# A float32 transformer kernel on one core: first layer woven with weight slabs in its attention; in the second layer weights split ahead of masks

## The chip, the cores and the metric

The kernel runs on one core of one Trainium2 chip, as a single launch. Its metric is the device time in microseconds (us) of that core. The engines are TensorE (PE in the profile; its weight loads are PEld), VectorE (DVE), ScalarE (ACT), GpSimd (POOL) and SyncE (SP), which here only issues transfers. TensorE runs at one of two clocks, 1.2 or 2.4 GHz; PEclk in the profile is the share of the upper one that was granted.

## The reference, cut to what matters

Two models follow each other on 512 tokens of width 1024, two layers each. The change is in the two layers of the first model, where every matrix is float32:

```python
for i in range(2):                       # first_block
    h = rmsnorm(x, norm_mix[i])
    ...                                  # mk, mv: keys and values of 256 memory tokens
    if i % 2 == 0:                       # first layer: 12 query heads, 4 key heads, 4 memory heads
        q, k, v, qm = jnp.split(h @ w_in_a[li], [qw, qw + kvw, qw + 2 * kvw], axis=-1)
        y_tok = windowed_gqa(...)        # 4 blocks of 128 queries, up to 384 keys, ALiBi, a sink logit
    else:                                # second layer: 12 query, 12 key heads
        q, k, v, qm = jnp.split(h @ w_in_b[li], [qw, 2 * qw, 3 * qw], axis=-1)
        y_tok = neighbourhood_attn(...)  # 256 keys, a learned bias per head (rpb), a grid mask
    y_mem = memory_attn(qm, mk, mv)
    x = x + jnp.concatenate([y_tok, y_mem], axis=-1) @ w_out[i]
    ...                                  # gated FFN
```

## The kernel before, in words

Activations lie with the model's width on the partitions, so a head pair of 64 + 64 columns is one "tile" of 128 partitions by 512 tokens. A "slab" is 128 output columns of a weight matrix, all 1024 rows: 128 x 1024 float32, 512 KB. float32 products are made from rounded parts. SP brings a slab to `raw` (a ring of two slots), ACT rounds it to `w_hi` (L987), POOL subtracts to get `w_lo` (L695), each in halves of 128x512, and PE makes three products for each of the 8 row tiles: hi by hi, lo by hi, hi by lo (L1466), 24 matmuls a slab and 12 a half slab. Each engine runs its own list in order; semaphores join them.

The first layer before: a projection of 12 slabs (queries, keys, values, memory queries), then the attention in 6 tiles of 4 query blocks, 24 "steps" (a step is one block of one tile, both heads), then 8 steps of memory attention, then the output projection of 8 slabs. Slabs and steps don't mix there.

The second layer is "woven": `woven_row` puts the 8 memory steps and the 24 neighbourhood steps in one row. In step p, PE makes the scores of p, the transposes of p-2, half a slab of the projection (`woven_part`, L1694 in `products`; a tile's query slab and key slab, 4 halves in 4 steps), and the values of p-3. After step 23 the projection is used up, and `OUT_PARTS` gives the steps 24 to 31 single row tiles of the first two output slabs. ACT in step p makes the exponentials of the first head (`probs`, L1088), copies the transposes of p-1 out of PSUM (`turned_woven`, L1195), makes those of the second head, rounds y (L1170), and rounds half a slab (`split_woven`). DVE adds the bias and takes the row maximum as it reads the scores (L2013). POOL in `attend_woven` does in each step, in this order: a chore, a half of `w_lo`, and `y_lo`. The chore stages a piece of the tile that comes four steps later: its queries (L723, L725), its keys, its values (L776), or, in every fourth step, its bias with the grid mask (`mask`, L790, three instructions), which the very next step's scores take:

```python
if p.at + 4 < len(row):
    then = row[p.at + 4]
    ...
    chores[then.st][n](then.tile)
if n < 2 and 1 <= u <= W_TILES:
    split_lo(first + u, 1, UP, (n,))
if n >= 2 and u < W_TILES:
    split_lo(first + u + 1, 0, UP, (n - 2,))
```

At the head of a woven row POOL waits until DVE has emptied both accumulators (`acc_free`) and then stages the first tile.

## Time and profile before

| | us |
|---|---|
| runs of the kernel | 2647.85, 2651.76, 2651.86 (median 2651.76) |
| the profiled execution | 2646.34 |
| its span in the trace | 2644.6 |
| first layer: projection | 52 to 121.3 |
| first layer: attention, memory attention | 121.3 to 188.0, 188.0 to 209.5 |
| first layer: output projection | 209.5 to 261.6 |
| second layer: woven row | 673 to 841 |

The times of the trace are us from the span's start. A row of a timeline gives the start, the time of the group, the engine, the line, the operation and its tiles; in brackets stands how long the engine had stood before, and whose end released it. The stretches of the table are read off PE's timeline, where its lines change.

### The profile page before, as it was taken

What the parts mean: (1) busy time and instruction counts of PE and PEld (TensorE: products, weight loads), DVE (VectorE), ACT (ScalarE), POOL (GpSimd) and SP (SyncE); (2) the same over time, 40 slices, a digit from 0 to 9 for tenths busy, and PEclk for the clock granted to TensorE, in tenths of its full rate; (3) what the DMA queues carried; (4) which work ended last, traced back from release to release, by engine and by line L of the source; (5) the groups of instructions that cost most, each with busy time, mean ns of one, the idle gap of its engine ahead of it and who ended that gap; (6) DMA issues with size and microseconds to landing.
All of it is one profiled execution on the core that took longest, in us unless ns stands there. A gap on an engine that the chain in (4) does not pass through costs nothing.

```text
span 2644.6 us, 46681 instructions
## 1 busy us (share of the span) xinstructions
PE 2541.5 (96%) x16758; PEld 2196.2 (83%) x16758; DVE 959.7 (36%) x1748; ACT 919.9 (35%) x1988; POOL 1201.3 (45%) x1039
## 2 busy tenths in 40 slices
PE   7999999999999999999998979999999888999999
PEld 7767888888776888888997869999999667998897
DVE  4263221223445221226753433422432543441341
ACT  4284322232244322234242223322233565322231
POOL 4554444444565444444442534444444443444443
PEclk9999999999999999999998989999999999999999
DMA  5211232232121222232221002232222100223222
GB/s 174 80 42 64 95 103 87 91 106 83 53 63 58 92 95 99 87 107 88 83 77 41 2 20 93 87 101 78 92 93 75 33 25 33 90 93 99 92 93 97
DMA packets 59473, 209.16 MB, mean 79 GB/s; under 512 B 8544, under 2 KB 11232, under 8 KB 59360
## 3 DMA queue, kind: packets, MB, share of 16 engines
q1 hardware_dynamic: 59360, 207.66, 24.1%
q8 instruction: 70, 1.15, 0.2%
q14 instruction: 43, 0.35, 0.0%
HBM read 205.54 MB, written 2.10 MB: 79 GB/s over the span
## 4 chain that ended last, share of the span: by engine, by line
PE 90%; DVE 4%; ACT 2%; issue 2%; POOL 1%; SPq 1%; DVEq 0%; DMA 0%; ACTq 0%; POOLq 0%
PE ps L1466 74%; PE ps L1694 3%; PE ps L1660 2%; PE ps L1642 1%; PE ps L1830 1%; PE ps L1591 1%; PE ps L1619 1%; PE ps L1819 1%; DVE s_sb L2013 1%; PE ps L1481 1%; PE ps L1669 1%; PE ps L1684 1%; DVE y_sb L1988 0%; DVE s_sb L1988 0%; PE ps L1604 0%
## 5 line engine op out<-in xcount | busy, mean ns | idle before, releaser
L695 POOL TENSOR_TENSOR w_lo<-raw,w_hi 128x512 fp32r<-128x512 f32 (+1 forms) x704 | 977.4, 1409 | 1156.1 <-ACT w_hi L987 1155.7
L987 ACT ACTIVATE w_hi<-raw 128x512 fp32r<-128x512 f32 (+1 forms) x704 | 428.2, 653 | 1276.0 <-PE ps L1466 1256.5
L1466 PE MATMUL ps<-h_hi,w_hi 128*128 128x264 f32 (+2 forms) x2832 | 791.4, 329 | 11.4 <-POOL h_lo L910 8.0
L1466 PE MATMUL ps<-h_lo,w_hi 128*128 128x264 f32 (+2 forms) x2832 | 789.5, 328 | 0.0
L1466 PE MATMUL ps<-h_hi,w_lo 128*128 128x264 f32 (+2 forms) x2832 | 786.8, 328 | 0.0
L1466 PEld LDWEIGHTS ps<-h_hi,w_hi 128*128 128x128 f32 x2832 | 479.8, 189 | 64.9 <-issue 13.8
L1466 PEld LDWEIGHTS ps<-h_lo,w_hi 128*128 128x128 f32 x2832 | 476.5, 189 | 48.1 <-issue 1.0
L1466 PEld LDWEIGHTS ps<-h_hi,w_lo 128*128 128x128 f32 x2832 | 476.7, 189 | 47.2
L1466 PE MATMUL ps<-act_lo,w_hi 128*128 128x512 f32 (+1 forms) x880 | 280.5, 351 | 0.0
L1466 PE MATMUL ps<-act_hi,w_lo 128*128 128x512 f32 (+1 forms) x880 | 279.8, 350 | 0.0
L1466 PE MATMUL ps<-act_hi,w_hi 128*128 128x512 f32 (+1 forms) x880 | 278.8, 349 | 0.0
L1988 DVE TENSOR_TENSOR x<-x,ps 128x512 f32<-128x512 f32 (+3 forms) x96 | 66.6, 693 | 432.0 <-PE ps L1466 430.5
L1466 PEld LDWEIGHTS ps<-act_hi,w_hi 128*128 128x128 f32 x880 | 153.3, 188 | 24.4
L1466 PEld LDWEIGHTS ps<-act_lo,w_hi 128*128 128x128 f32 x880 | 153.6, 188 | 24.0
L1466 PEld LDWEIGHTS ps<-act_hi,w_lo 128*128 128x128 f32 x880 | 153.9, 188 | 22.7
L1988 DVE TENSOR_TENSOR ps<-gated,ps 128x512 f32<-128x512 f32 (+1 forms) x88 | 61.6, 701 | 169.4 <-PE ps L1466 169.1
L1983 DVE SCALAR_TENSOR_TENSOR ps<-padded,vec,ps 128x528 f32<-128x528 f32 (+1 forms) x132 | 101.2, 767 | 25.9 <-issue 15.5
L1988 DVE TENSOR_TENSOR act_lo<-ps,act_hi 128x512 f32 (+1 forms) x88 | 61.2, 696 | 104.3 <-ACT act_hi L1252 104.3
L1988 DVE TENSOR_TENSOR padded<-ps,rstd 128x528 f32<-128x528 f32 (+1 forms) x56 | 39.4, 703 | 154.8 <-PE ps L1466 143.6
L1983 DVE SCALAR_TENSOR_TENSOR h_lo<-x,vec,h_hi 128x512 fp32r<-128x512 f32 (+2 forms) x64 | 59.4, 928 | 81.2 <-ACT h_hi L994 68.1
L1249 ACT ACTIVATE ps<-ps 128x512 f32<-128x512 f32 (+1 forms) x88 | 51.5, 585 | 105.8 <-DVE ps L1983 105.8
L1988 DVE TENSOR_TENSOR gated<-ps,rstd 128x512 f32<-128x512 f32 (+1 forms) x88 | 61.2, 696 | 73.2 <-ACT ps L1249 73.2
(311 smaller groups left out, 2785.0 us busy)
## 6 DMA issues: line engine op xcount, KB each, us to landing
raw<-slabs_d SPq DMA_DIRECT2D x288, 512.0 KB, 3.3
raw<-slabs_d SPq DMA_DIRECT2D x64, 704.0 KB, 4.0
bias_sb<-alibi_d SPq DMA_DIRECT2D x6, 384.0 KB, 3.7
x<-x_d SPq DMA_DIRECT2D x1, 2048.0 KB, 13.5
out_d<-x SPq DMA_DIRECT2D x8, 256.0 KB, 4.4
rpb_raw<-rpb_d SPq DMA_DIRECT2D x6, 256.0 KB, 2.7
mem_in<-mem_d SPq DMA_DIRECT2D x1, 1024.0 KB, 7.2
cst<-consts_d SPq DMA_DIRECT2D x1, 792.0 KB, 9.4
```

The costliest lines, as they stand in the source:

```text
L695: nc.gpsimd.tensor_tensor(w_lo[:, s, a * P:b * P], raw[:, s, a * P:b * P], w_hi[:, s, a * P:b * P].bitcast(f32), ALU.subtract).then_inc(lo ...
L987: nc.scalar.activation(w_hi[:, s, a * P:b * P], raw[:, s, a * P:b * P], ACT.Copy)\
L1249: nc.scalar.activation(acc(2, st.used), acc(2, st.used), ACT.Silu).then_inc(silu_ready, 1)
L1466: last = nc.tensor.matmul(ps[:, s * 2 * BANK + po:s * 2 * BANK + po + n], w[:, s, wk], columns(a, k, to, n), start=(k == 0 and w is w_hi a ...
L1481: last = nc.tensor.matmul(out, a[:, k, t0:t0 + n], w[:, s, wk], start=(k == 0 and w is w_hi and a is hi), stop=(k == DT - 1 and w is w_lo))
L1591: last = nc.tensor.matmul(p.score(h)[0:p.nq, col:col + n], a[hp, p.tile_slot, p.q], b[hp, p.tile_slot, k0:k0 + n], start=(b is k_hi and a ...
L1619: last = nc.tensor.transpose(to, s_sb[0:p.nq, p.slot, h, 1 + col:1 + col + n], ident[0:p.nq, 0:p.nq])
L1642: last = nc.tensor.matmul(split_acc[:, c, :], wt[:, w.s, k * P:(k + 1) * P], a[:, k, to:to + n], start=(k == 0 and wt is w_hi and a is hi) ...
L1660: nc.tensor.matmul(out[HD * h:HD * h + HD, 0:p.nq], v_st[0:n, p.tile_slot, vb, HD * h:HD * h + HD], p_t[0:n, p.slot, h, j, 0:p.nq], start= ...
L1694: last = nc.tensor.matmul(acc(s, 1), w[:, s, k * P:(k + 1) * P], columns(a, k, META, SEQ), start=(k == first and w is w_hi and a is hi), s ...
L1983: return nc.vector.scalar_tensor_tensor(*a, **kw)
L1988: return nc.vector.tensor_tensor(*a, **kw)
```

## The change

In the first layer the projection keeps 4 slabs (two of memory queries, two of values). The rest is woven like the second layer: memory attention comes first, in steps 0 to 7, and beside it the slabs of the first two query tiles and of the two key tiles; then come the 24 windowed steps. Three query tiles share one key tile there (`group=3`), so of a tile only one query slab is left to make, which stands as two halves in the even steps. The odd steps have no slab. Output slab parts stand in steps 24 to 28 and 31 (`OUT_FIRST`), the rest behind the last step. The transposes of the second head go to another PSUM bank. In ACT's step `spread` and `move_y`, which the windowed attention needs for its sums, stand between the second head's exponentials and y.

In both layers POOL now splits its half slab ahead of the chore, waits for only one accumulator before it stages the first tile, and `OUT_PARTS` is ordered anew.

```diff
-    proj(10, 2, 1)
-    out[-1].queries = (0, 1, 2, 4)
+    proj(2, 2, 1)
+    out[-1].queries = (0,)
+    out[-1].woven = True
+    att(nt=2, blocks=m_blocks, bias=None, sink=None, qt=0, kt=0, group=1, y=6, layer=0)
+    out[-1].woven = True
+    slabs(2 * 2, UP)
     att(nt=6, blocks=a_blocks, bias="alibi", sink=0, qt=0, kt=6, group=3, y=0, layer=0)
-    att(nt=2, blocks=m_blocks, bias=None, sink=None, qt=8, kt=0, group=1, y=6, layer=0)
-    tail(2, 1, 0, False, (3, 1))
+    out[-1].woven = True
+    slabs(4, UP)
...
-        OUT_PARTS = {24: [(0, 6), (0, 7)], 25: [(0, 0), (0, 1)], 26: [(0, 2)], 27: [(1, 6), (1, 7)], 28: [(1, 0)],
-                     29: [(1, 1)], 30: [(1, 2)], 31: [(0, 3)]}
+        OUT_FIRST = {24: [(0, 0)], 25: [(0, 1)], 26: [(0, 2)], 27: [(0, 6)], 28: [(0, 7)], 31: [(0, 3)]}
+        def woven_slab(a, p):
+            first, u, n = a.slab0 // 2, p.at // 4, p.at % 4
+            if u >= W_TILES:
+                return None
+            if u < 2 or not shares_keys(a):
+                return first + u, n // 2, range(n % 2 * DT // 2, (n % 2 + 1) * DT // 2), n // 2
+            if n % 2:
+                return None
+            return first + 2 + (u - 2) // 2, u % 2, range(n // 2 * DT // 2, (n // 2 + 1) * DT // 2), 0
+        def shares_keys(a):
+            return stages[stages.index(a) + 1].group > 1
+        def out_pair(a):
+            return a.slab0 // 2 + (4 if shares_keys(a) else W_TILES)
+        def woven_splits(a, p):
+            first, u, n = a.slab0 // 2, p.at // 4, p.at % 4
+            if n < 2:
+                if u == 1 or (u <= W_TILES and u and not shares_keys(a)):
+                    return [(first + u, 1, n)]
+                return [(out_pair(a), 1, n)] if u == W_TILES else []
+            if u >= W_TILES:
+                return []
+            if not shares_keys(a) or u == 0:
+                return [(first + u + 1, 0, n - 2)]
+            return [(first + 2 + (u - 1) // 2, 1 - u % 2, n - 2)]
+        OUT_PARTS = {24: [(0, 0), (0, 1)], 25: [(0, 2)], 26: [(0, 6), (0, 7)], 27: [(1, 0), (1, 1)], 28: [(1, 2)],
+                     29: [(1, 6)], 30: [(1, 7)], 31: [(0, 3)]}
...
-                for s in range(RING):
-                    pool.wait_ge(acc_free[s], first)
+                pool.wait_ge(acc_free[0], first)
                 for n in (0, 1, 2):
                     chores[a][n](0)
+                pool.wait_ge(acc_free[1], first)
                 stream(a.slab0 + 2)
                 pool.wait_ge(val_kept, a.val0)
                 for p in row:
                     u, n = p.at // 4, p.at % 4
+                    for q, s, part in woven_splits(a, p):
+                        split_lo(q, s, UP, (part,))
                     if p.at + 4 < len(row):
                         then = row[p.at + 4]
                         if then.st is b and n < 2:
-                            pool.wait_ge(acc_free[n], first + then.tile + 1)
+                            if then.tile < 2 or not shares_keys(a):
+                                pool.wait_ge(acc_free[n], first + then.tile + 1)
+                            elif n == 0:
+                                pool.wait_ge(acc_free[then.tile % 2], first + 2 + (then.tile - 2) // 2 + 1)
                         chores[then.st][n](then.tile)
-                    if n < 2 and 1 <= u <= W_TILES:
-                        split_lo(first + u, 1, UP, (n,))
-                    if n >= 2 and u < W_TILES:
-                        split_lo(first + u + 1, 0, UP, (n - 2,))
                     if p.back(3).exists:
                         y_lo_of(p.back(3).st, p.back(3).tile, p.back(3).b)
                 for p in row[-3:]:
                     y_lo_of(p.st, p.tile, p.b)
...
+                        act.wait_ge(pv_done, p.count - 1)
+                    if p.st.sink is not None:
+                        n = len(p.c["chunks"])
+                        for h in range(2):
+                            last = nc.scalar.activation(
+                                p_t[:, p.slot, h, 0:n, :],
+                                bank(4 - 2 * h)[:, 0:n * P].rearrange("p (c n) -> p c n", n=P), ACT.Copy)
+                        last.then_inc(pt_ready[0], 1)
+                        return
...
                         probs(p, 1)
+                        if p.back(1).exists:
+                            spread(p.back(1))
+                        if p.back(2).exists:
+                            move_y(p.back(2))
                         if p.back(3).exists:
                             y_hi(p.back(3))
                         split_woven(p)
...
+                    if p.st.sink is not None:
+                        pe.wait_ge(acc_free[1], st.slab0 // 2 + 2)
                     for j, (col, n, _) in enumerate(p.c["chunks"]):
...
                 def woven_part(p):
-                    u, n = p.at // 4, p.at % 4
-                    if u >= W_TILES:
-                        out_parts(OUT_PARTS[p.at])
+                    if woven_slab(st, p) is None:
+                        out_parts((OUT_FIRST if shares_keys(st) else OUT_PARTS).get(p.at, []))
                         return
-                    q, s, half = st.slab0 // 2 + u, n // 2, n % 2
-                    if half:
+                    q, s, tiles, at = woven_slab(st, p)
+                    if tiles[0] == 0:
+                        begin(q, s)
+                        if s != at or (shares_keys(st) and p.at >= 8):
+                            pe.wait_ge(acc_free[1 - s], q + s)
+                    if tiles[0] == DT // 2:
                         second_half(q, s)
-                    else:
-                        begin(q, s)
-                    products(q, s, range(half * DT // 2, (half + 1) * DT // 2), h_hi[st.h], h_lo[st.h], 0, DT - 1)
+                    products(s, at, tiles, h_hi[st.h], h_lo[st.h], 0, DT - 1)
```

Three places show it as the engines' lists have it. POOL, second layer, step 6 to 7 (`v_st` is the values' chore of tile 0, `bias_sb` its mask, `y_w` a y_lo). Before:

```order
L776 COPY v_st<-val_w_80 128x640
L695 TENSOR_TENSOR w_lo<-raw,w_hi 128x512
L810 TENSOR_TENSOR y_w_0_82<-y_sb_w_81,y_w_0_82 128x128
L790 TENSOR_TENSOR bias_sb<-rpb_raw,cst 128x2x256
L790 TENSOR_TENSOR bias_sb<-rpb_raw,cst 128x2x192 x2
L695 TENSOR_TENSOR w_lo<-raw,w_hi 128x512
L810 TENSOR_TENSOR y_w_1_83<-y_sb_w_81,y_w_1_83 128x128
```

After:

```order
L736 TENSOR_TENSOR w_lo<-raw,w_hi 128x512
L817 COPY v_st<-val_w_60 128x640
L851 TENSOR_TENSOR y_w_0_62<-y_sb_w_61,y_w_0_62 128x128
L736 TENSOR_TENSOR w_lo<-raw,w_hi 128x512
L831 TENSOR_TENSOR bias_sb<-rpb_raw,cst 128x2x256
L831 TENSOR_TENSOR bias_sb<-rpb_raw,cst 128x2x192 x2
L851 TENSOR_TENSOR y_w_1_63<-y_sb_w_61,y_w_1_63 128x128
```

The mask was ahead of its step's `w_lo` and is now behind it; so are the other chores.

ACT, first layer, one windowed step (`p_t` is the copy of transposes, `s_sb,p_sum` the exponentials). Before:

```order
L1103 ACTIVATE p_t<-ps 128x256
L1091 ACTIVATE s_sb,p_sum<-s_sb,n_max 128x385
L1103 ACTIVATE p_t<-ps 128x256
L1091 ACTIVATE s_sb,p_sum<-s_sb,n_max 128x385
L1147 ACTIVATE p_rec<-p_inv 128x128
L1157 ACTIVATE y_sb_55<-ps 128x128
L1170 ACTIVATE h_hi_49<-y_sb_55 128x128
```

After, in a step that has half a slab:

```order
L1131 ACTIVATE s_sb,p_sum<-s_sb,n_max 128x385
L1241 ACTIVATE p_t<-ps 128x384 x2
L1131 ACTIVATE s_sb,p_sum<-s_sb,n_max 128x385
L1189 ACTIVATE p_rec<-p_inv 128x128
L1199 ACTIVATE y_sb_w_61<-ps 128x128
L1212 ACTIVATE y_w_2_64<-y_sb_w_61 128x128
L1029 ACTIVATE w_hi<-raw 128x512
```

The copies moved from between heads to ahead of the second head's exponentials, and the rounding of half a slab stands last.

PE, first layer, a windowed step (`k_hi,q_hi` are scores, `cst,s_sb` transposes, `p_t,v_st` values). Before:

```order
L1591 MATMUL ps<-k_hi,q_hi 128x256 x2
L1591 MATMUL ps<-k_lo,q_hi 128x256 x2
L1591 MATMUL ps<-k_hi,q_lo 128x256 x2
L1604 MATMUL ps<-cst,s_sb 128x128 x6
L1660 MATMUL ps<-p_t,v_st 64x128 x6
L1675 MATMUL ps<-cst,p_rec 128x128
```

After, from the last row tile of a half slab on:

```order
L1756 MATMUL ps<-h_hi_49,w_hi 128x512
L1756 MATMUL ps<-h_lo_50,w_hi 128x512
L1756 MATMUL ps<-h_hi_49,w_lo 128x512
L1716 MATMUL ps<-p_t,v_st 64x128 x4
L1731 MATMUL ps<-cst,p_rec 128x128
L1647 MATMUL ps<-k_hi,q_hi 128x256 x2
L1647 MATMUL ps<-k_lo,q_hi 128x256 x2
L1647 MATMUL ps<-k_hi,q_lo 128x256 x2
L1747 MATMUL ps<-cst,s_sb 128x128 x6
L1716 MATMUL ps<-p_t,v_st 64x128 x4
L1731 MATMUL ps<-cst,p_rec 128x128
L1647 MATMUL ps<-k_hi,q_hi 128x256 x2
```

The transposes of a step with no slab are followed at once by the values of the step before, and then the next scores.

## Rows read from the trace of the kernel before

**Rows 1.** The page, part 1: busy time of each engine, its share of the span, instructions.

```profile
PE 2541.5 (96%) x16758; PEld 2196.2 (83%) x16758; DVE 959.7 (36%) x1748; ACT 919.9 (35%) x1988; POOL 1201.3 (45%) x1039
```

**Rows 2.** Windows of the first layer: window, length, busy time of each engine (instructions), PEclk.

```profile
121.30:188.00 66.70, 61.65 (x550) 42.64 (x550) 46.54 (x171) 58.96 (x221) 40.11 (x60) 0.95 0.14 44
188.00:209.50 21.50, 16.80 (x186) 13.05 (x186) 13.94 (x22) 11.73 (x37) 4.57 (x10) 0.92 0.01 2
209.50:262.00 52.50, 52.43 (x219) 42.13 (x219) 17.06 (x24) 18.61 (x34) 24.04 (x16) 0.97 0.24 76
```

**Rows 3.** Timeline of PE, second layer, steps 8 and 9: where their scores start.

```profile
777.16 0.36 PE L1591 MATMUL ps<-k_hi,q_hi 64*128 64x192 f32 x2
...
782.07 0.39 PE L1591 MATMUL ps<-k_hi,q_hi 64*128 64x256 f32 x2
```

**Rows 4.** Timeline of POOL, second layer: a mask and the halves of w_lo behind masks.

```profile
776.66 3.22 POOL L790 TENSOR_TENSOR bias_sb<-rpb_raw,cst 128x512 f32<-128x512 f32 x3
780.27 1.28 POOL L695 TENSOR_TENSOR w_lo<-raw,w_hi 128x512 fp32r<-128x512 f32 x1 [0.39 <-ACT w_hi L987]
...
800.84 1.26 POOL L695 TENSOR_TENSOR w_lo<-raw,w_hi 128x512 fp32r<-128x512 f32 x1 [0.37 <-ACT w_hi L987]
```

**Rows 5.** Timeline of DVE, second layer, step 8: the scores' first head.

```profile
779.92 0.36 DVE L2013 CUSTOM_DVE_ANT_0 s_sb<-ps,bias_sb 128x192 f32<-128x192 f32 x1 [1.32 <-POOL bias_sb L790]
```

**Rows 6.** Timeline of ACT, second layer, step 8.

```profile
778.36 0.60 ACT L1195 ACTIVATE p_t<-ps 128x512 f32<-128x512 f32 x1 [3.15 <-PE ps L1684]
...
779.56 0.64 ACT L987 ACTIVATE w_hi<-raw 128x512 fp32r<-128x512 f32 x1
```

**Rows 7.** Timeline of PE, second layer: the stands of the row's end, and what followed.

```profile
802.36 0.70 PE L1694 MATMUL ps<-y_w,w_hi 128*128 128x512 f32 x2 [3.41 <-POOL w_lo L695]
...
803.89 0.63 PE L1694 MATMUL ps<-y_w,w_lo 128*128 128x512 f32 x1
...
806.36 0.51 PE L1591 MATMUL ps<-k_hi,q_hi 64*128 64x256 f32 x2
...
841.50 0.73 PE L1466 MATMUL ps<-y_w,w_hi 128*128 128x512 f32 x2 [1.43 <-POOL w_lo L695]
842.07 0.40 PE L1466 MATMUL ps<-y_w,w_lo 128*128 128x512 f32 x1
```

**Rows 8.** Timeline of PE at the head of the woven row.

```profile
676.26 0.39 PE L1591 MATMUL ps<-k_hi,q_hi 64*128 64x256 f32 x2 [3.55 <-POOL k_lo L725]
...
677.74 0.80 PE L1694 MATMUL ps<-h_hi,w_hi 128*128 128x512 f32 x1 [0.86 <-POOL w_lo L695]
```

**Rows 9.** Timeline of DVE at the head of the woven row: the copy of the values.

```profile
672.99 1.27 DVE L1998 COPY val_w<-ps 128x384 f32<-128x384 f32 x3
```

**Rows 10.** Timeline of POOL at the head of the woven row.

```profile
673.02 0.61 POOL L723 CAST q_hi<-ring 128x512 fp32r<-128x512 f32 x1 [9.73 <-issue]
```

**Rows 11.** Timeline of PE, first layer: one step, its values, the next scores.

```profile
137.38 0.39 PE L1591 MATMUL ps<-k_hi,q_hi 64*128 64x256 f32 x2
...
138.80 0.66 PE L1660 MATMUL ps<-p_t,v_st 128*64 128x128 f32 x8
...
139.65 0.38 PE L1591 MATMUL ps<-k_hi,q_hi 64*128 64x256 f32 x2
```

**Rows 12.** Timeline of ACT, first layer: from one step into the next.

```profile
139.69 0.50 ACT L1103 ACTIVATE p_t<-ps 128x384 f32<-128x384 f32 x1
140.06 0.63 ACT L1091 ACTIVATE s_sb<-s_sb,n_max 128x385 f32<-128x385 f32 x1
...
141.22 0.51 ACT L1103 ACTIVATE p_t<-ps 128x384 f32<-128x384 f32 x1
```

**Rows 13.** Timeline of DVE, first layer: two copies of the sink logits.

```profile
121.38 1.29 DVE L1988 TENSOR_TENSOR s_sb<-neg_rows 128x2 f32<-128x2 f32 x1
...
149.28 0.16 DVE L1988 TENSOR_TENSOR s_sb<-neg_rows 128x2 f32<-128x2 f32 x1
```

**Rows 14.** Timeline of POOL, first layer, beside the first of these copies.

```profile
121.36 2.51 POOL L695 TENSOR_TENSOR w_lo<-raw,w_hi 128x512 fp32r<-128x512 f32 x2 [1.66 <-ACT w_hi L987]
```

More of the change, by code:

```diff
@@ L837, in attend_woven @@
                     y_lo_of(p.st, p.tile, p.b)
-                streamed(2 * (first + W_TILES) + 2)
+                streamed(2 * out_pair(a) + 2)
             def attend(st, nxt, nv):
@@ L1076, in attend @@
             def attend(st):
-                off = 1 if st.sink is None else 0
                 def probs(p, h):
@@ L1140, in spread @@
                 def spread(p):
-                    if st.summed:
+                    if p.st.summed:
                         return
+                    if p.row and p.back(2).exists and p.back(2).st.summed:
+                        act.wait_ge(y_ready, p.count - 1)
                     act.wait_ge(inv_ready, p.kept + 1)
@@ L1198, in split_woven @@
                 def split_woven(p):
-                    first, u, n = st.slab0 // 2, p.at // 4, p.at % 4
-                    if n < 2 and 1 <= u <= W_TILES:
-                        split_hi(first + u, 1, UP, (n,))
-                    if n >= 2 and u < W_TILES:
-                        split_hi(first + u + 1, 0, UP, (n - 2,))
+                    for q, s, part in woven_splits(st, p):
+                        split_hi(q, s, UP, (part,))
                 if st.woven:
@@ L1215, in attend @@
                     turned_woven(last)
-                    for k in (2, 1, 0):
-                        y_hi(last.back(k))
+                    spread(last)
+                    move_y(last.back(1))
+                    y_hi(last.back(2))
+                    move_y(last)
+                    y_hi(last.back(1))
+                    y_hi(last)
                     return
@@ L1680, in turn_woven, with products @@
                     pe.wait_ge(p_ready, 2 * p.count + 2)
-                    pe.wait_ge(pt_ready[0], p.count)
+                    if counted(p.count):
+                        pe.wait_ge(pt_ready[0], p.count)
+                    if p.st.sink is not None:
+                        pe.wait_ge(acc_free[1], st.slab0 // 2 + 2)
                     for j, (col, n, _) in enumerate(p.c["chunks"]):
                         for h in range(2):
-                            last = nc.tensor.transpose(bank(4)[0:n, (2 * h + j) * P:(2 * h + j + 1) * P],
-                                                       s_sb[0:p.nq, p.slot, h, 1 + col:1 + col + n], ident)
+                            if p.st.sink is not None:
+                                to = bank(4 - 2 * h)[0:n, j * P:(j + 1) * P]
+                            else:
+                                to = bank(4)[0:n, (2 * h + j) * P:(2 * h + j + 1) * P]
+                            last = nc.tensor.transpose(to, s_sb[0:p.nq, p.slot, h, 1 + col:1 + col + n], ident)
                     last.then_inc(pt_done, 2)
                 transpose = turn_woven if st.woven else turn_both if st.mixed else turn
-                def products(q, s, tiles, hi, lo, first, end):
+                def products(s, at, tiles, hi, lo, first, end):
                     for k in tiles:
                         for w, a in ((w_hi, hi), (w_hi, lo), (w_lo, hi)):
-                            last = nc.tensor.matmul(acc(s, 1), w[:, s, k * P:(k + 1) * P], columns(a, k, META, SEQ),
+                            last = nc.tensor.matmul(acc(at, 1), w[:, s, k * P:(k + 1) * P], columns(a, k, META, SEQ),
                                                     start=(k == first and w is w_hi and a is hi),
@@ L2249, in attend @@
                         scores(p)
+                        if p.back(1).exists:
+                            invert(p.back(1))
                         evict_woven(p)
```

59 lines of the change are left out of this document (37 added, 22 removed).

## The prediction

> **What bounds the kernel now.** Read the page's first part first: PE is busy for 96% of the span [rows 1], so an edit counts only where PE stands, or where it runs at the lower clock. The windows of the first layer show where that is. In the attention PE has 61.65 of 66.70 us and ACT 58.96, so ACT nearly fills that stretch; in the memory attention PE has 16.80 of 21.50; in the output projection 52.43 of 52.50 [rows 2]. PE thus stands 5.05 + 4.70 + 0.07 = 9.8 us. The granted clocks 0.95, 0.92 and 0.97 on these lengths are (0.05 x 66.7) + (0.08 x 21.5) + (0.03 x 52.5) = 3.3 + 1.7 + 1.6 = 6.6 us more, if all of it is time. So 16.4 us is all that weaving can give back. In the second layer PE's timeline has stands only at the head of the woven row (3.55 and 0.86 us) [rows 8], once where its steps lose their half slab (3.41, released by `w_lo`) and at its end (1.43) [rows 7]. The masks cost nothing there yet: at step 8 the scores start on PE at 777.16 and those of step 9 at 782.07 [rows 3], while DVE reads the first head of step 8 at 779.92, released by the mask [rows 5]. The mask is late for DVE by 1.32, and DVE still frees the PSUM bank (779.92 + 0.36 = 780.28) 1.8 us before PE asks for it again.
>
> **Second layer: the mask behind `w_lo`.** POOL did the mask at 776.66, for 3.22 us, then waited 0.39 for ACT and made `w_lo` from 780.27, 1.28 long [rows 4]. That half cannot start sooner when it stands first: its `w_hi` starts on ACT at 779.56 and takes 0.64, and it comes behind a copy of transposes which PE makes only after the scores of the next step (ACT stood 3.15 for them, until 778.36) [rows 6]. So `w_hi` of a step ends 779.56 + 0.64 - 777.16 = 3.04 us into PE's next step, and everything behind it on POOL is later than that. The new order gives `w_lo` 780.27 to 781.55, the mask 781.55 to 784.77, DVE's first head to 784.77 + 0.40 = 785.17. PE's scores of step 9 want to start at 782.07 and use that bank: a stand of 785.17 - 782.07 = 3.1 us. What waits behind the mask on POOL is a `y_lo`, which the output needs much later; what waits behind DVE is ACT's exponentials, and by them the transposes two steps on, which have slack of a step. The stand comes for every mask made while PE still has half slabs beside it: tiles 0 to 3, so 4 x 3.1 = 12.4.
>
> Tile 4 is where the half slabs end. There the old order made PE stand 3.41 for the `w_lo` behind the mask (at 800.84) [rows 4, 7]. The new `OUT_PARTS` takes row tiles of the first half there, which is ready, so this stand goes, and the mask is late instead: with a shorter step beside it by an estimated 3.9. I take 0 for the two together. Tile 5 has no half slab behind which to stand, but its step is short; I take +1.3, from the same order of slack (1.32) [rows 5].
>
> A stand also cost clock. Behind the one of 3.41 a matmul of 128x512 took 0.63 at 803.89, behind the one of 1.43 it took 0.40 at 842.07 [rows 7]: half clock after the long one, none after the short one. From 803.89 to the scores at 806.36, which took 0.51 where 0.39 is usual [rows 3, 7], 2.47 us passed at roughly 0.40/0.63 of the speed, or half, which is 0.9 to 1.3 lost; I take 1.3. Four new stands of 3.1 are nearer to 3.41 than to 1.43: 4 x 1.3 = 5.2, with bounds 0 and, if the low clock lasts twice as long, 10.4.
>
> The head of the row gains. POOL's staging started at 673.02, after the copy of the values on DVE began (672.99, three pieces in 1.27) and nine microseconds idle [rows 9, 10]. It waited for both accumulators, and needs only the first now, which DVE empties while PE still makes the last slab. PE itself waits for the values' copy, so its scores can start about when that ends, 672.99 + 1.27 = 674.26, and after scores that take 0.7 the first product, at 677.74 before [rows 8], stands near 675.0: -2.7, and about -1 for a shorter stretch at half clock, so -3.7. It can't be sooner than the values' copy; the other bound is 0, if POOL's `w_lo` of the last slab takes the place of the wait.
>
> Sum for the second layer: 12.4 + 0 + 1.3 + 5.2 - 3.7 = +15. With the clock's bounds and the head's it is +7.5 to +20.
>
> **First layer.** The same number of slabs and steps is made, so only what PE stood counts. ACT's work per windowed step is, from two copies of transposes at 0.37 each (139.69 to 140.06), two heads of exponentials, 0.63 each, of which the second with three small ones behind it takes 1.16 (140.06 to 141.22) [rows 12], 2.5 us (0.74 + 0.63 + 1.16), and 0.64 for the half slab in some steps [rows 6]. A step on PE without a slab is 139.65 - 137.38 = 2.27 [rows 11]; a half slab adds 12 matmuls, at 52.43 / 219 = 0.24 [rows 2] 2.9. Over the two kinds PE needs 3.7 a step and ACT at most 3.14, so ACT no longer bounds the mean, and most of the 16.4 goes. What stays or comes:
>
> - at the head, 1.5 (the values' copy, as above, ends 1.5 behind PE's last product);
> - a wait for `w_lo` in steps 12, 16, 20 and 24. Those halves are split in the even step two before, and between is one step without a slab. Behind the end of the transposes, 138.80 - 137.38 = 1.42 into the light step [rows 11], ACT does two copies 0.74, the second head and the small ones 1.16, and `w_hi` 0.64, then POOL `w_lo` 1.28: 1.42 + 0.74 + 1.16 + 0.64 + 1.28 = 5.24 us into that step. The product is due after 2.27 + 1.42 = 3.69. The wait is 1.55, with a hand-over 1.6: 6.4 in all;
> - DVE's copy of the sink logits, in front of each step's scores. At 121.38 it took 1.29, at 149.28 0.16 [rows 13]; beside the long one POOL's `w_lo` ran from 121.36 [rows 14]. In the woven steps `w_lo` stands on POOL near these copies. By the short row it costs 0, by the long one up to 1.1 in each of the 8 to 12 steps with a split, if DVE is what PE waits for; I take 3 times 0.8, 2.4;
> - the end, 1.4, as in the second layer's row [rows 7]; and about 1 of clock.
>
> By the Trainium skill ("SBUF — State Buffer", section "SBUF: two separate sides") VectorE and GpSimd share a port pair under an exclusive lock, and a two-input VectorE operation and a GpSimd one block each other for the whole instruction. The two copy rows agree with it, since the long copy ends within 0.1 us of the first of POOL's two instructions (121.36 + half of 2.51 = 122.62, the copy at 122.67). By that rule every copy that falls on a `w_lo` is held, and the term would be nearer 8 than 2.4, for which the first layer's sum would be about +2.
>
> The new sum is 1.5 + 6.4 + 2.4 + 1.4 + 1 = 12.7 against 16.4: about -3.5. Its bounds are -13 (only head and end stay, 1.5 + 1.4) and +4 (the copies held in every step, and the waits with clock lost behind them).
>
> **Sum.** +15 - 3.5 = about +12. The profiled execution took 2646.34 with a span of 2644.6, so it would be 2658; on the median of the runs, 2651.76, it would be 2664. I say 2661, between them, and take 5.3 us (0.2%) as what a measurement of this kernel can tell from no change.
>
> **Rivals.**
>
> *The mask is not late.* If ACT's `w_hi` comes sooner in the new program, or PE's scores need not the bank that waits for the mask, the second layer has only its gains: -3.4 (the stand at the end of the half slabs) - 1.3 (its clock) - 3.7 = about -8, and with the first layer's -3.5 the sum is -11 or so: 2640 by the median, 2636 to 2641. For it: DVE had 1.8 us of slack to PE. Against it: the 0.39 that POOL waited after the mask [rows 4], which shows that the old order had `w_hi` no earlier. 0.13.
>
> *The first layer gives nearly everything back,* -13, and the masks stand without losing clock, +10: about -3, 2648, no change. For it: ACT falls from 88% of its stretch to less than PE's share. Against it: the 1.55 us, made of durations in rows. 0.17.
>
> *Worse than forecast:* each stand is followed by the longer stretch of low clock, 10.4 rather than 5.2, and DVE's copies are held as far as the bound, +4 instead of -3.5: +12 + 5.2 + 7.5 = about +25, 2676. It decides if stands of 3.1 us are always followed by matmuls of 0.63. 0.08.
>
> *The forecast,* slower by 5 to 20 us (2657 to 2672): 0.62.
>
> **The numbers.** The range reaches from the middle of the second rival to the near side of the worse one, 2645 to 2675, and leaves out the first rival and half of the last. Faster by over 0.2%: the first rival, and a little of the second, 0.15. Within 0.2%: the rest of the second and the forecast's low end, 0.17. Slower: 0.68.
>
> **What would show it.** In the second layer, four stands of some 3 us on PE at the scores that follow a mask, released by DVE, with DVE released by POOL's mask; no stand of 3.41 for `w_lo`; the first product of the woven row 2 to 3 us nearer to the last product before it. In the first layer, four stands of 1 to 2 us for `w_lo` at the steps 12, 16, 20 and 24, and ACT well below PE. If PE's stands at the masks are under 1 us, the forecast is wrong in its main term; if the first layer's stands together are under 5, the second rival is right.

## The result, and the profile after

The changed kernel took 2671.63 us (median of 5; 2666.25 to 2684.64) against 2651.76 (median of 5): a ratio of 1.0088, 95% interval 1.0073 to 1.0104. It is slower, by 19.9 us. Single runs of 2809.15 (E1), 3960.47 (E4) and 2804.02 us (the kernel before) went at a much lower granted clock (0.84, 0.58 and 0.93) and are left out of the ratios here and below. The forecast had the sign, and a little under half the size: 2661, which is 9.2 over the median, on a sum of +12.

PE's two matmuls on `sq_sum` (part of a norm) stand once near the head of each layer's projection and once near the head of its FFN, so they cut both traces at the same places of the program. Windows between them, before (window, length, busy time of each engine, PEclk, DMA share, GB/s; first layer, second layer, second model):

```profile
57.45:261.14 203.69, 193.13 (x1227) 148.01 (x1226) 87.22 (x231) 103.25 (x314) 100.94 (x112) 0.97 0.19 63
629.42:880.08 250.66, 239.73 (x1537) 182.24 (x1536) 114.62 (x240) 94.73 (x202) 141.53 (x146) 0.98 0.20 65
1250.03:2644.60 1394.57, 1328.25 (x10479) 1227.40 (x10477) 540.96 (x961) 468.40 (x1024) 593.25 (x517) 0.97 0.22 71
```

and after:

```profile
58.84:265.55 206.71, 191.03 (x1228) 144.00 (x1227) 92.47 (x239) 103.63 (x306) 99.98 (x112) 0.98 0.19 62
633.86:897.49 263.63, 242.68 (x1537) 184.55 (x1536) 114.43 (x240) 94.96 (x202) 140.92 (x146) 0.97 0.18 62
1267.45:2667.10 1399.65, 1333.52 (x10479) 1230.30 (x10477) 540.81 (x961) 468.26 (x1024) 592.52 (x517) 0.97 0.22 71
```

The first layer is 3.0 us longer, the second 13.0. The FFNs between repeat within 0.04 us. The start (1.4 longer) and the second model (5.1 longer) hold nothing that was edited; they are taken up with E4, E8 and E9. Length less busy time is what PE stood: 10.6 to 15.7 us in the first layer, 10.9 to 21.0 in the second.

PE's timeline after, second layer: the head of the row, then the scores behind the masks of tiles 0, 4 and 5 (a bracket is the time that PE stood, and what released it; those of tiles 1 to 3 are 2.96 each), and one matmul behind the first of these masks:

```profile
678.78 0.39 PE L1647 MATMUL ps<-k_hi,q_hi 64*128 64x256 f32 x2 [1.60 <-DVE val_w L2068]
...
722.45 0.39 PE L1647 MATMUL ps<-k_hi,q_hi 64*128 64x256 f32 x2 [2.83 <-DVE n_max L2083]
...
724.04 0.63 PE L1756 MATMUL ps<-h_lo,w_hi 128*128 128x512 f32 x1
...
822.32 0.58 PE L1647 MATMUL ps<-k_hi,q_hi 64*128 64x256 f32 x2 [4.34 <-DVE n_max L2083]
...
838.32 0.39 PE L1647 MATMUL ps<-k_hi,q_hi 64*128 64x256 f32 x2 [0.80 <-DVE n_max L2083]
```

These answer to [rows 3, 7, 8]: four new stands of about 3, the 3.41 for `w_lo` gone and 4.34 behind the mask in its place, and the head of the row down from 3.55 + 0.86 to 1.60. The chain of the first one, ACT:

```profile
716.88 0.63 ACT L1029 ACTIVATE w_hi<-raw 128x512 fp32r<-128x512 f32 x1
```

then POOL:

```profile
717.58 1.28 POOL L736 TENSOR_TENSOR w_lo<-raw,w_hi 128x512 fp32r<-128x512 f32 x1 [2.56 <-ACT w_hi L1029]
718.82 3.17 POOL L831 TENSOR_TENSOR bias_sb<-rpb_raw,cst 128x512 f32<-128x512 f32 x3
```

then DVE, which stood 5.73 for the mask where it had stood 1.32 [rows 5]:

```profile
722.03 0.36 DVE L2083 CUSTOM_DVE_ANT_0 s_sb<-ps,bias_sb 128x192 f32<-128x192 f32 x1 [5.73 <-POOL bias_sb L831]
```

What [rows 3 to 6] call steps 8 and 9 are steps 20 and 21 by PE's list, at the mask of tile 3; the scores of step 8 start at 715.66 there, and DVE stood 1.29 for its mask. The steps repeat, so the reading holds.

POOL had nothing to do for 2.56 us ahead of `w_lo`, most of the 3.17 that the mask takes. In the first layer, PE's stands after (the one of 1.55 is there three times, that of 0.81 to 0.83 three times):

```profile
132.44 0.50 PE L1756 MATMUL ps<-h_hi,w_hi 128*128 128x512 f32 x1 [0.96 <-POOL w_lo L736]
...
141.32 0.44 PE L1647 MATMUL ps<-k_hi,q_hi 64*128 64x384 f32 x2 [0.81 <-DVE n_max L2083]
...
151.68 0.50 PE L1756 MATMUL ps<-h_hi,w_hi 128*128 128x512 f32 x1 [1.55 <-POOL w_lo L736]
...
202.72 0.39 PE L1647 MATMUL ps<-k_hi,q_hi 64*128 64x256 f32 x2 [2.93 <-POOL k_lo L766]
...
226.90 0.74 PE L1522 MATMUL ps<-y_w,w_hi 128*128 128x512 f32 x2 [1.45 <-POOL w_lo L736]
```

The `w_lo` stands are as long as worked out from [rows 11, 12]. The one for `k_lo` was in no forecast. POOL there, in the last tile's step 24 to 25:

```profile
196.65 1.28 POOL L766 TENSOR_TENSOR q_lo<-ring,q_hi 128x512 fp32r<-128x512 f32 x1
197.88 0.46 POOL L851 TENSOR_TENSOR y_gap<-y_sb_w,y_gap 128x128 fp32r<-128x128 f32 x1
199.50 1.27 POOL L736 TENSOR_TENSOR w_lo<-raw,w_hi 128x512 fp32r<-128x512 f32 x1 [1.16 <-ACT w_hi L1029]
200.72 0.61 POOL L764 CAST k_hi<-ring 128x512 fp32r<-128x512 f32 x1
201.41 1.26 POOL L766 TENSOR_TENSOR k_lo<-ring,k_hi 128x512 fp32r<-128x512 f32 x1
```

POOL waits 1.16 for ACT and then makes a half slab that nobody needs yet, and the keys, for which PE stands, come after it.

### The profile page after: what moved, and what is told of

It is laid out like the page before. It is cut to its first block, busy times and chain, and to the rows that moved or that the text cites. A ratio compares the mean times of both kernels' runs of the same rounds, so it can differ in the third digit from the quotient of the medians.

```text
span 2667.1 us, 46373 instructions
## 1 busy us (share of the span) xinstructions
PE 2548.7 (96%) x16758; PEld 2198.3 (82%) x16758; DVE 964.6 (36%) x1756; ACT 920.2 (35%) x1980; POOL 1198.4 (45%) x1039
## 4 chain that ended last, share of the span: by engine, by line
PE 89%; DVE 3%; POOL 3%; ACT 2%; issue 2%; DMA 0%; DVEq 0%; SPq 0%; ACTq 0%; POOLq 0%
PE ps L1522 72%; PE ps L1756 4%; PE ps L1716 2%; PE ps L1647 1%; PE ps L1698 1%; PE ps L1900 1%; PE ps L1747 1%; PE ps L1675 1%; POOL w_lo L736 1%; PE ps L1889 1%; PE ps L1537 1%; POOL bias_sb L831 1%; PE ps L1725 0%; ACT w_hi L1029 0%; PE ps L1721 0%
## 5 line engine op out<-in xcount | busy, mean ns | idle before, releaser
L1522 PE MATMUL ps<-h_hi,w_hi 128*128 128x264 f32 (+2 forms) x2704 | 739.3, 325 | 8.1 <-POOL h_lo L952 8.0
L1522 PE MATMUL ps<-h_lo,w_hi 128*128 128x264 f32 (+2 forms) x2704 | 737.3, 325 | 0.0
L1522 PE MATMUL ps<-h_hi,w_lo 128*128 128x264 f32 (+2 forms) x2704 | 735.7, 324 | 0.0
L1522 PEld LDWEIGHTS ps<-h_hi,w_hi 128*128 128x128 f32 x2704 | 455.3, 189 | 55.9 <-issue 10.4
L1522 PEld LDWEIGHTS ps<-h_lo,w_hi 128*128 128x128 f32 x2704 | 451.3, 188 | 42.4 <-issue 1.0
L1522 PEld LDWEIGHTS ps<-h_hi,w_lo 128*128 128x128 f32 x2704 | 451.9, 189 | 41.6
```

Of the source, the lines that this page charges most:

```text
L1522: last = nc.tensor.matmul(ps[:, s * 2 * BANK + po:s * 2 * BANK + po + n], w[:, s, wk], columns(a, k, to, n), start=(k == 0 and w is w_hi a ...
```

## The experiments

Lengths are those of the windows between the `sq_sum` matmuls, of the profiled execution; the fourth layer is the second model's second, and its attention, projections included, is a part of the second model's length. The median is of all runs. The ratio of an experiment is to the kernel before as it was run beside it (medians 2649.79 for E1 to E4, 2647.51 for E5 to E7, 2646.29 for E9 and E10), so it is not the quotient of two medians of this table.

| kernel | first layer | second layer | second model | of it fourth layer's attention | median | ratio to before |
|---|---|---|---|---|---|---|
| before | 203.69 | 250.66 | 1394.57 | 258.07 | 2651.76 | |
| changed | 206.71 | 263.63 | 1399.65 | 261.64 | 2671.63 | 1.0088 (1.0073 to 1.0104) |
| E1 chores first | 203.24 | 240.66 | 1411.60 | 274.80 | 2653.90 | 0.9998 (0.9980 to 1.0017) |
| E2 mask first | 206.61 | 240.89 | 1411.17 | 274.81 | 2657.26 | 1.0016 (0.9999 to 1.0033) |
| E3 before, new order on POOL | 202.48 | 271.89 | 1397.09 | 258.22 | 2671.75 | 1.0090 (1.0073 to 1.0106) |
| E4 early rounding | 192.07 | 240.64 | 1412.13 | 274.80 | 2643.47 | 0.9962 (0.9946 to 0.9979) |
| E5 one-input copy | 202.42 | 267.53 | 1390.37 | 251.94 | 2676.78 | 1.0108 (1.0093 to 1.0122) |
| E6 both of these | 191.15 | 239.07 | 1389.90 | 251.93 | 2628.12 | 0.9938 (0.9921 to 0.9955) |
| E7 E4, second model later | 192.03 | 239.12 | 1412.31 | 274.81 | 2677.02 | 1.0088 (1.0064 to 1.0112) |
| E8 before again | 204.14 | 250.68 | 1398.63 | 258.13 | 2653.04 (one run) | |
| E9 changed again | 206.75 | 266.30 | 1413.33 | 274.80 | 2675.61 | 1.0098 (1.0082 to 1.0115) |
| E10 all three | 191.12 | 239.17 | 1393.51 | 254.48 | 2624.47 | 0.9913 (0.9900 to 0.9926) |

**E1: POOL's chores ahead of the half slab again.** In the changed kernel's `attend_woven`:

```diff
-                    for q, s, part in woven_splits(a, p):
-                        split_lo(q, s, UP, (part,))
                     if p.at + 4 < len(row):
...
                         chores[then.st][n](then.tile)
+                    for q, s, part in woven_splits(a, p):
+                        split_lo(q, s, UP, (part,))
```

> The changed kernel, with POOL's chore ahead of its half slab again, in both layers; all else of the change stays. If the order on POOL is the cause: no stand of 3 us at the scores behind a mask (five of them, 16 us, in the changed kernel), and the stand of 2.93 for k_lo at 202.7 in the first layer goes; the second layer takes about 246 us instead of 263.6 (between its marks on sq_sum), the first about 203.5 instead of 206.7; 2648 to 2653 in all. If the time lies in stretches that the change doesn't touch (start and second model, 6.5 of the 22.5 us between the two profiles): both layers stay within 3 us of the changed kernel and the time is 2665 to 2672.

No stand at a mask is left, 0.50 is left where PE stood for `k_lo`, and both layers came out lower than forecast for them, 203.24 and 240.66. The order on POOL cost 3.5 us in the first layer and 23.0 in the second: 16.9 of stands (21.0 to 4.1), the rest lower clock. The two layers are 10.5 us shorter than before the change, but the median isn't: the profiled run took 2655.64, and its second model is 17.0 longer than in the kernel before, 16.7 of it in the fourth layer's attention. The times of E1 lie in two groups, 2637.92 to 2641.91 (four) and 2652.50 to 2658.36 (seven); those of E2 too, 2642.07 to 2647.35 (four) and 2656.48 to 2661.75 (eight). The lower group of E1 is where the layers alone would put it, 2651.76 - 10.5 = 2641.3.

**E2: the mask alone ahead.** Chore 3 moves ahead of the half slab, the others stay behind it:

```diff
+                    early = n == 3 and p.at + 4 < len(row)
+                    if early:
+                        chores[row[p.at + 4].st][n](row[p.at + 4].tile)
                     for q, s, part in woven_splits(a, p):
                         split_lo(q, s, UP, (part,))
-                    if p.at + 4 < len(row):
+                    if p.at + 4 < len(row) and not early:
```

> The changed kernel, with only the mask ahead of its step's half slab; queries, keys and values stay behind it. If the mask alone makes the second layer's stands: that layer takes about 246 us as with all chores first, the first layer stays at 206.7 with its 2.93 for k_lo; about 2651 to 2656. If the other chores matter too in the second layer: it stays above 250.

The second layer is that of E1 in length, 240.89, and shorter than expected; the first is that of the changed kernel, and the median is 1.3 above the expected range. The stands behind the masks of tiles 0 to 4 are gone but for one of 0.22; behind the mask of tile 5 one of 1.45 is left, which E1 doesn't have, and PE lost less to lower clock than there (235.1 busy against 236.6). So the mask alone makes nearly all of the second layer's loss. The 2.93 of the first layer, and what clock went with it, belong to the other chores; the row that releases PE there names the keys.

**E3: the new order in the kernel before.**

```diff
                     u, n = p.at // 4, p.at % 4
+                    if n < 2 and 1 <= u <= W_TILES:
+                        split_lo(first + u, 1, UP, (n,))
+                    if n >= 2 and u < W_TILES:
+                        split_lo(first + u + 1, 0, UP, (n - 2,))
                     if p.at + 4 < len(row):
...
                         chores[then.st][n](then.tile)
-                    if n < 2 and 1 <= u <= W_TILES:
-                        split_lo(first + u, 1, UP, (n,))
-                    if n >= 2 and u < W_TILES:
-                        split_lo(first + u + 1, 0, UP, (n - 2,))
```

> The kernel before, with one edit: POOL splits its half slab ahead of the chore in the woven row of the second layer. If the order on POOL is the cause: stands of about 3 us on PE behind five masks, the second layer 250.7 + 15 = about 266 us, the first layer as before, 203.7; about 2665 to 2670. If the stands in the changed kernel need the first layer's weaving or the new order of output parts: under 255 us, 2650 to 2656.

The same four stands, 2.84 to 2.97, without the weaving of the first layer; and the 3.41 stays, since the old `OUT_PARTS` still asks for the second half there:

```profile
725.05 0.39 PE L1591 MATMUL ps<-k_hi,q_hi 64*128 64x256 f32 x2 [2.84 <-DVE n_max L2013]
...
823.16 1.19 PE L1694 MATMUL ps<-y_w,w_hi 128*128 128x512 f32 x2 [3.41 <-POOL w_lo L695]
```

The second layer is 6 us longer than expected, 271.89, and the median lies above the range: PE stands 23.7 there, 12.7 more than before, and lower clock cost 8.5 more (248.2 busy against 239.7).

**E4: rounding early on ACT.** POOL's new order stays.

```diff
                         probs(p, 0)
+                        split_woven(p)
                         if p.back(1).exists:
                             turned_woven(p.back(1))
...
-                        split_woven(p)
```

> The changed kernel, with POOL's order kept, but ACT rounds its half slab right behind the first head's exponentials, ahead of the copy of transposes. If w_hi's place behind PE's transposes is why the mask and w_lo come late: w_hi comes some 4 us sooner, the five stands at masks go (second layer about 246 us), and in the first layer the stands for w_lo (0.96 and three of 1.55) and for k_lo (2.93) go, about 198 us; 2640 to 2646 in all, faster than before. If POOL has too much to do, wherever w_hi stands: the stands at the masks stay above 2 us and the time above 2660.

The rival, that POOL has too much to do, falls. ACT at the first mask of the second layer:

```profile
699.84 0.64 ACT L1029 ACTIVATE w_hi<-raw 128x512 fp32r<-128x512 f32 x1
703.35 0.60 ACT L1246 ACTIVATE p_t<-ps 128x512 f32<-128x512 f32 x1 [2.87 <-PE ps L1747]
```

POOL:

```profile
700.56 1.29 POOL L736 TENSOR_TENSOR w_lo<-raw,w_hi 128x512 fp32r<-128x512 f32 x1 [0.42 <-ACT w_hi L1029]
701.80 3.22 POOL L831 TENSOR_TENSOR bias_sb<-rpb_raw,cst 128x512 f32<-128x512 f32 x3
```

ACT fills a gap in which it had stood for PE's transposes, and POOL's `w_lo` starts 1.6 us ahead of the scores of the step at 702.15 instead of 3 behind them. DVE waits 1.21 for the mask, as it did before the change, and PE not at all. In the first layer the four `w_lo` stands and the three at 0.8 are gone, 0.47 is left of the one for `k_lo`, and PEclk is 1.00. At 192.07 it is 6 us better than expected: the three copies of the sink logits that had taken 1.05 beside a `w_lo` take 0.28 to 0.29, which is the 2.5 of PE's stands, and PE's busy time fell from 191.03 to 186.78 with the clock. The two layers are 21.6 us shorter than before, but the median only 6.3 against the runs beside it: the second model took 1412. In its fourth layer's attention, which no edit reaches, some 58 us went at half the clock; 50 of them (same columns as the windows above):

```profile
2170.47:2220.47 50.00, 45.97 (x223) 32.08 (x222) 10.38 (x47) 18.25 (x69) 6.04 (x12) 0.50 0.04 11
```

The same stretch of the kernel before, by its distance from the second model's start:

```profile
2190.00:2240.00 50.00, 44.84 (x371) 36.94 (x371) 16.10 (x55) 25.10 (x84) 13.46 (x18) 0.98 0.10 33
```

It isn't that the kernel before had no low clock in that layer: in windows of 5 us it shows several shorter stretches, two of them, some 10 and 7 us long, in the 40 us ahead of this window and at its start. By the granted clock of these windows the layer's attention went at half clock for some 24 us in all before, 34 in the changed kernel and 72 in E4. Between the marks on `sq_sum` it took 258.07 before, 261.64 in the changed kernel and 274.80 in E4. Before:

```profile
2015.56:2273.63 258.07, 232.99 (x1913) 196.49 (x1911) 105.06 (x332) 136.71 (x440) 111.00 (x144) 0.95 0.13 42
```

In the changed kernel:

```profile
2034.75:2296.39 261.64, 237.54 (x1912) 199.40 (x1911) 104.98 (x332) 136.61 (x440) 110.77 (x144) 0.93 0.13 41
```

**E5: DVE's copy of the sink logits with one input**, in the changed kernel:

```diff
-                        tt(s_sb[:, p.slot, :, 0:1], sink, sink, ALU.max)
+                        reduce(s_sb[:, p.slot, :, 0], sink, AX.X, ALU.max)
```

> The changed kernel; in the first layer DVE's copy of the sink logits (a maximum of the two columns with themselves, two inputs in SBUF) becomes a reduction with one input; same values. If the copy is held because of its two inputs, the copies at 139.47 and 174.80, 1.05 long beside a w_lo on POOL, take about 0.2, and PE's three stands of 0.81 to 0.83 behind n_max in the first layer go: 204.3 instead of 206.7 there. If anything on DVE is held while POOL makes w_lo: no difference. The second layer stays at 263.6; in all 2666 to 2670.

The expectation overlooked that the fourth layer's attention uses the same line: its 40 copies took 17.0 us in the changed kernel and 6.3 here, and it is down from 261.64 to 251.94. In the first layer, DVE's 24 copies of the changed kernel and of E5 (count, busy time, mean ns):

```profile
L2058 DVE TENSOR_TENSOR s_sb<-neg_rows 128x2 f32<-128x2 f32 x24 | 9.6, 402 | 9.1 <-PE ps L1747 8.0 <-issue 0.2
```

```profile
L2078 DVE TENSOR_REDUCE s_sb<-neg_rows 128x2 f32<-128x2 f32 x24 | 3.8, 157 | 9.7 <-PE ps L1747 8.7 <-issue 0.2
```

The three stands of 0.8 are gone and the layer is 4.3 us shorter, 1.9 more than expected (less lower clock too). The rival, that anything on DVE is held while POOL makes `w_lo`, falls. The median, 2676.78, is above the expected range. The profiled run is the one of 2659.31, 9.6 less than that of the changed kernel, nearly all of it in the second model; its second layer took 267.53, with the same 21 us of stands. The other four took 2675.46 to 2677.36; where their 16 to 18 us went, no profile shows.

**E6: early rounding and the one-input copy.**

> The early rounding of half slabs on ACT and the one-input copy together. Early rounding has left 4.4 us of stands in the first layer and 4.1 in the second, none longer than 0.23 behind DVE, so the copy should be worth nothing more: 192 and 240.6 us, 2640 to 2645 in all. If held copies still cost time beside longer w_lo: 190 or less in the first layer.

Less is left in the first layer than the forecast of no gain, 191.15 against 192.07, and the median is 15 us lower than E4's, 12 below the expected range. Of the 25.6 us between the two profiled runs (2618.74, E6's lowest, and 2644.36), 22.2 lie in the second model (1389.90, granted clock 0.97 against 0.95), whose fourth layer has the one-input copy and no long stretch at half clock.

**E7: the second model later.** E4 with repeats of one matmul ahead of the second layer's FFN:

```diff
-                for po, to, n in chunks(nm.blk):
+                for po, to, n in chunks(nm.blk) * (44 if nm.n == 4 else 1):
```

> The early rounding, and 43 repeats of one matmul (sum of squares, same result) ahead of the second layer's FFN, some 10 to 20 us, so that the second model starts at about the time at which it did in the kernel before. In the profile with early rounding the fourth layer's attention, which no edit touches, ran 50 us at a granted clock of 0.50, and the times lie in two groups 15 us apart. If the start of that attention in time decides on this: no such stretch, times in one group, about 2640 to 2650. If not: the repeats are added, 2655 to 2665, and two groups remain.

The repeats took 36.9 us, not 10 to 20, so the second model started at 1266.1, as in the changed kernel (1267.5), and not at the 1250 of the kernel before that was aimed at, and the time is above the expected range. Two groups remain: 2661.02 and 2662.35, and 2674.81 to 2680.22 four times. So one program falls into both (the profiled runs of E1, E2, E4 and E7 are all of the longer group), and the start time doesn't sort the profiles either: the long stretch is there at 1230.5 (E4), 1242.2 (E1), 1245.0 (E2), 1266.1 (E7) and 1270.8 (E9), and not at 1250.0 (before), 1252.7 (E8), 1267.5 (changed) and 1272.8 (E3).

**E8: the kernel before, once more.**

> The kernel before, once more, for a second profile. What no edit touches should repeat: first layer 203.7, second 250.7, FFNs 368.3 and 370.0. By how much the start (57.5) and the second model (1394.6) differ is what two profiles of one program differ by.

First and second layer repeat within 0.5 us; the start took 59.63 instead of 57.45, and the second model 4.1 us longer, 4.4 of it in the third layer's attention (276.93 and 281.36). So the 1.4 by which the changed kernel's start was longer is no more than two profiles of one program differ by. The second model's 5.1 is only in part: the fourth layer's attention repeats, 258.07, 258.13, and 258.22 in E3, while with the newly woven first layer and the same copy it took 261.64 once and 274.80 or 274.81 five times. In this first layer PE stood 0.82 and 0.81 behind `n_max`, just after copies of 1.20 and 1.17, so copies are held in the kernel before too, and not in the same steps in every run. The layer has 12.8 of stands where the first profile had 10.6, less lower clock, and nearly the same length.

**E9: the changed kernel, once more.**

> The changed kernel, once more. The stands should repeat: 15.3 us in the first layer, 20.9 in the second. If what is left of the layers' time, PE's lower clock behind the stands, differs from run to run, the second layer lies between 263 and 272 (it was 263.6 in the changed kernel, 267.5 with one DVE operation of the first layer changed, 271.9 in the kernel before with the new order on POOL) and the time between 2665 and 2685. If it is fixed: 206.7 and 263.6 again.

First layer 206.75 again, stands again 14.9 and 20.9 (brackets of 0.2 and more; 15.3 and 20.9 the first time). The second layer took 266.30 at a PEclk of 0.96, so the clock behind equal stands isn't fixed, and this time the second model had the long stretch at half clock, 274.80 in the fourth layer's attention and 2685.85 in all for that run:

```profile
2210.77:2260.77 50.00, 45.96 (x226) 31.82 (x223) 10.38 (x47) 19.21 (x72) 7.11 (x13) 0.50 0.03 11
```

**E10: all three edits** (E1, E4 and E5 in one kernel).

> Early rounding on ACT, the one-input copy, and POOL's chores ahead of the half slab as before the change. If w_hi's place on ACT is the cause of the stands, the order on POOL is worth nothing once w_hi comes early: first layer 191, second 239 to 241, as with early rounding and the one-input copy alone, 2620 to 2640. If the order still matters: the half slabs that now stand behind a mask of 3.2 us are late, stands for w_lo of 1 us or more appear in the second layer.

With `w_hi` early the order on POOL is worth nothing in the layers (191.12 and 239.17, as E6), and no `w_lo` stand came but the one at the end that all have (1.44). At 2624.47, five runs within 2.7 us, it is 0.9% faster than the kernel before, and PE runs both layers at full clock:

```profile
59.24:250.36 191.12, 186.46 (x1228) 141.88 (x1226) 86.53 (x239) 103.10 (x306) 100.66 (x112) 1.00 0.21 68
618.67:857.84 239.17, 235.07 (x1538) 179.27 (x1537) 114.40 (x240) 94.58 (x202) 141.92 (x146) 1.00 0.21 68
```

That gives the layers' work at full clock, 186.5 and 235.1 us, and with it an estimate of what lower clock cost elsewhere: PE's busy time less this. For the kernel before it takes as given that as many matmuls (1227 and 1537) are as much work.

## Why the prediction was right in its sign and short in its size

*Masks behind `w_lo`: right.* Forecast 4 x 3.1; measured 2.83 and three times 2.96, 11.7. Tile 4: forecast 3.9 for 3.41; measured 4.34 for 3.41, +0.9. Tile 5 forecast +1.3, measured 0.80 less the 0.26 that stood near there for `w_lo`, +0.5. E3 gives the stands without the rest of the change, E2 takes all but the last away by moving the mask alone. The list of stands before left out one of 1.40 for `y_r` near the row's end (838.41); it became 1.05.

*Head of the row: right.* Stands of 4.41 became 1.60, -2.8 against the -2.7 worked out from the values' copy.

*Clock behind the stands of the second layer: right in size on two profiles, not a fixed price.* The steps behind the four masks were 5.7 us longer than usual together in both profiles of the changed kernel, forecast 5.2 (7.2 in E3, 8.6 in E5). Over the layer, lower clock cost 239.7 - 235.1 = 4.6 us before, and 7.6 and 10.3 in the two profiles of the changed kernel, with the same stands; 13.1 in E3. The forecast had +5.2 less 1 at the head; +3.0 and +5.7 were measured. So the second layer is +13.0 and +15.6 in two pairs of profiles, forecast +15 (bounds 7.5 to 20).

*First layer: wrong, and this is the step that failed.* Forecast -3.5, measured +3.0 and +2.6. The baseline was right: 10.6 of stands and 193.1 - 186.5 = 6.6 of clock before, forecast 9.8 and 6.6. So, nearly, were the listed terms: head 1.13 (1.5), `w_lo` 0.96 + 3 x 1.55 = 5.6 (6.4), DVE's held copies 3 x 0.82 = 2.5 (2.4), end 1.45 (1.4). What the sum lacked stands in three places. The new order on POOL was priced only where a mask is behind it; in the first layer the keys of the last tile are behind it too, where the steps have grown short: a stand of 2.93, and with its clock 3.4 to 3.5 (E1 against the changed kernel, E2 as the control). Lower clock was put at 1 without a row, and is 191.03 - 186.46 = 4.6. Short stands of 0.74, 0.38, 0.36 and 0.22 were not listed, 1.7 together, nor 0.4 of shorter ones. That is 2.9 + 3.6 + 1.7 + 0.4 = 8.6 missed, less 1.1 by which the listed terms were too high (11.7 for 10.6): 7.5. Against it stand 6.7 by which the layer is longer than the sum (12.7 - 16.4 = -3.7, rounded to -3.5) and 0.8 of stands that the baseline lacked.

*The point: too low on top of it.* The layers' sum, 16.0 to 18.2, on the median of 2651.76 gives 2668 to 2670; the forecast took a point between the profiled execution and the median, 2.8 us under its own sum on the median. What is left of the measured 19.9 is 2 to 4 us, and the forecast had put all that lies outside the two layers at nothing. In the profiles the fourth layer's attention is 3.6 us longer in the changed kernel, and 16.7 with the long stretch at half clock. So the range held its median with some luck: five of the changed kernel's eleven runs took over 2675. Why kernels with the newly woven first layer run the fourth layer's attention longer with the same copy, though each engine's list there is the same, and show the long stretch in five of nine profiles, while none of the three with the old first layer does, stays open. The start time doesn't sort them (E7). In E5, E6 and E10, where the copy has one input in the fourth layer too, the profile shows none of the long stretch, but E6's times still spread over 22 us, and four of E5's five runs are 16 to 18 us longer than the profiled one.

*The rivals.* "The mask is not late" has the second layer's size right for a program in which it is not: -8 forecast, -10.0 in E1. "Gives nearly everything back" is what the first layer does with early rounding: -11.6 in E4, -12.6 in E10, bound -13. Neither is what this change does. "Worse than forecast" has the first layer's bound, +4, nearly right, by the keys and the clock and not by held copies; its stretch of low clock behind every stand, 10.4, is more than the 5.7 of the changed kernel.

*The port.* By the Trainium skill ("SBUF — State Buffer", section "SBUF: two separate sides") a VectorE operation with two inputs in SBUF and a GpSimd operation that reads SBUF block each other for a whole instruction. The trace and E5 agree: beside a `w_lo` the copy took 1.05, the one-input operation 0.16 at the same place. In the changed kernel:

```profile
139.23 1.27 POOL L736 TENSOR_TENSOR w_lo<-raw,w_hi 128x512 fp32r<-128x512 f32 x1 [5.87 <-ACT w_hi L1029]
139.47 1.05 DVE L2058 TENSOR_TENSOR s_sb<-neg_rows 128x2 f32<-128x2 f32 x1 [0.72 <-PE ps L1747]
```

In E5:

```profile
137.75 1.28 POOL L736 TENSOR_TENSOR w_lo<-raw,w_hi 128x512 fp32r<-128x512 f32 x1 [4.30 <-ACT w_hi L1029]
137.98 0.16 DVE L2078 TENSOR_REDUCE s_sb<-neg_rows 128x2 f32<-128x2 f32 x1 [0.71 <-PE ps L1747]
```

The term's price was nearer the one taken from the rows: the 24 copies were 5.8 us longer than E5's together, but PE stood for only 2.8 of it, three times 0.82 and once 0.36. That the first layer came out near the rule's +2 is chance.

## What to carry to other kernels

When two pieces of work on one engine change places, price every piece that is now behind, not only the largest: for each, who takes it next and how soon, in the steps where the others have grown short. Before reordering the engine that is late, look at what releases it: here POOL stood idle 2.6 us for a rounding that ACT did behind a wait for PE, and moving that one line (E4) was worth 14.6 and 23.0 us in the two layers of the changed kernel; the order on POOL makes no difference then (E6 and E10). Compare layers between marks that both programs have, those that nobody edited too, and run the kernel before a second time, or a gain can hide in such a stretch.

## What was not expected of the hardware

The same stands cost PE different amounts of lower clock: 7.6, 10.3 and, in E5, 246.6 - 235.1 = 11.5 us in the second layer, at 21 us of stands each. The price comes in sizes: behind the 16 stands of 2.83 to 2.97 at masks in four profiles (changed, E3, E5, E9), the step that usually takes 4.95 was 1.5 to 1.6 us longer nine times, 2.6 to 2.8 five times, and no longer twice. Two stands of 2.96 in the changed kernel, with a matmul of the step behind each:

```profile
772.42 0.39 PE L1647 MATMUL ps<-k_hi,q_hi 64*128 64x256 f32 x2 [2.96 <-DVE n_max L2083]
...
773.72 0.40 PE L1756 MATMUL ps<-h_lo,w_hi 128*128 128x512 f32 x1
...
796.09 0.58 PE L1647 MATMUL ps<-k_hi,q_hi 64*128 64x256 f32 x2 [2.96 <-DVE n_max L2083]
...
798.37 0.63 PE L1756 MATMUL ps<-h_lo,w_hi 128*128 128x512 f32 x1
```

And in the fourth layer's attention, with the same lists and no stand of PE over 1.9 us, the clock was at half for some 24, 34 or 72 us in all, which goes with lengths of 258.1, 261.6 and 274.8. In the long stretch PE was busy for 46 of 50 us at a granted clock of 0.50.
